# Prompt attention: each unit's two softmax maps are combined between the maxima of the next unit, the first map's sum is carried into the row norm's epsilon, and outputs are copied from PSUM

## The reference

```python
s = einsum('bqhcd,bkhcd->bhcqk', q, k) * scale      # c: the two maps
s = where(dist >= 0, s + bias, -inf)                # causal, ALiBi
p = softmax(s, axis=-1)
a = p[:, :, 0] - lam * p[:, :, 1]
oa = einsum('bhqk,bkhd->bqhd', a, v)
oa = oa * rsqrt(mean(oa * oa, -1) + EPS) * g_oa * (1 - lam_init)
ua = (oa * silu(az)) @ w_branch[0]
```

## Time and profile before

| | us |
|---|---|
| median of 3 runs | 1460.74 |
| lowest, highest | 1460.13, 1461.68 |
| profiled execution, its own time | 1461.76 |
| its span | 1459.8 |
| TensorE busy in the span | 1335.7 |
| VectorE, ScalarE busy | 559.4, 465.2 |

### The profile page before, as it was taken

One profiled execution on the slowest core, in us unless ns is written; L12 is line 12 of the kernel. 1 busy time (PEld: TensorE's weight loads), 2 busy tenths in 40 slices (PEclk: granted clock), 3 DMA queues, 4 the chain that ended last, 5 costly groups with the idle time before them and its releaser, 6 DMA issues.

```text
span 1459.8 us, 19287 instructions
## 1 busy us (share of the span) xinstructions
PE 1335.7 (91%) x7822; PEld 1145.7 (78%) x7822; DVE 559.4 (38%) x1174; ACT 465.2 (32%) x1025; POOL 107.1 (7%) x124
## 2 busy tenths in 40 slices
PE   6999999878787899988769989999999999999998
PEld 5788779656566785867657768778899999999776
DVE  5654334565564324245553334332223222221511
ACT  5543222454444324334442234321222111221300
POOL 0000000000000000000010000000012222221110
PEclk9999999898899999998978989999999999999999
DMA  8340111000002430101111220333111113110422
GB/s 284 112 161 2 58 48 44 15 15 15 0 15 56 159 117 31 30 15 30 44 55 40 62 98 23 109 109 105 44 44 44 44 44 102 44 44 22 144 89 70
DMA packets 89833, 94.41 MB, mean 65 GB/s; under 512 B 8450, under 2 KB 64530, under 8 KB 89618
## 3 DMA queue, kind: packets, MB, share of 16 engines
q1 hardware_dynamic: 85410, 79.28, 17.7%
q0 software_dynamic: 4336, 13.90, 2.6%
HBM read 79.27 MB, written 13.89 MB: 64 GB/s over the span
## 4 chain that ended last, share of the span: by engine, by line
PE 83%; DVE 7%; ACT 6%; issue 4%; DMA 1%; SPq 0%; POOLq 0%; POOL 0%; DVEq 0%; ACTq 0%
PE heavy L813 13%; PE heavy L814 13%; PE heavy L815 13%; PE heavy L825 8%; PE heavy L826 8%; PE heavy L827 8%; PE heavy L870 4%; PE attended L940 2%; ACT arena L1439 2%; PE scores L920 1%; PE transposed L929 1%; PE scores L1173 1%; PE scores L1076 1%; PE transposed L897 1%; PE attended L1190 1%
## 5 line engine op out<-in xcount | busy, mean ns | idle before, releaser
L1332 ACT ACTIVATE arena<-heavy 128x364 f32<-128x364 f32 (+1 forms) x108 | 51.0, 472 | 416.2 <-PE heavy L815 416.2
L813 PE MATMUL heavy<-h_hi,rc_hi 128*128 128x364 f32 (+1 forms) x384 | 134.6, 351 | 2.1 <-DVE arena L2087 2.1
L814 PE MATMUL heavy<-h_lo,rc_hi 128*128 128x364 f32 (+1 forms) x384 | 129.6, 338 | 0.0
L815 PE MATMUL heavy<-h_hi,rc_lo 128*128 128x364 f32 (+1 forms) x384 | 129.3, 337 | 0.0
L813 PE MATMUL heavy<-h_hi,rp_hi 128*128 128x364 f32 (+1 forms) x384 | 126.3, 329 | 0.0
L814 PE MATMUL heavy<-h_lo,rp_hi 128*128 128x364 f32 (+1 forms) x384 | 126.1, 328 | 0.0
L815 PE MATMUL heavy<-h_hi,rp_lo 128*128 128x364 f32 (+1 forms) x384 | 126.1, 328 | 0.0
L1766 DVE SCALAR_TENSOR_TENSOR arena<-arena,heavy 128x364 f32<-128x364 f32 (+1 forms) x48 | 25.5, 532 | 214.1 <-PE heavy L815 214.1
L595 POOL TENSOR_TENSOR merged<-merged,arena 128x364 f32<-128x364 f32 (+1 forms) x48 | 67.1, 1399 | 442.2 <-DVE arena L1766 442.2
L813 PEld LDWEIGHTS heavy<-h_hi,rc_hi 128*128 128x128 f32 x384 | 75.8, 197 | 15.2 <-issue 11.7
L814 PEld LDWEIGHTS heavy<-h_lo,rc_hi 128*128 128x128 f32 x384 | 75.7, 197 | 0.0
(11 more groups left out here) (312 smaller groups left out, 2982.2 us busy)
## 6 DMA issues: line engine op xcount, KB each, us to landing
out<-arena POOLq DMA_DIRECT2D x36, 256.0 KB, 3.3
rc_whole<-w_in SPq DMA_DIRECT2D x16, 512.0 KB, 3.8
rp_whole<-w_in SPq DMA_DIRECT2D x16, 512.0 KB, 4.0
arena<-x_prompt SPq DMA_DIRECT2D x8, 512.0 KB, 5.6
arena<-cache_k_a SPq DMA_DIRECT2D x16, 256.0 KB, 3.0
arena<-cache_v_a SPq DMA_DIRECT2D x16, 256.0 KB, 3.3
ra_whole<-w_in SPq DMA_DIRECT2D x8, 512.0 KB, 4.1
arena<-cache_mem_k SPq DMA_DIRECT2D x8, 512.0 KB, 4.7
```

The source lines that it names most:

```text
L813: nc.tensor.matmul(out, a_hi, b_hi, start=(x == 0), stop=False)
L814: nc.tensor.matmul(out, a_hi, b_lo, start=False, stop=False)
L815: end = nc.tensor.matmul(out, a_lo, b_hi, start=False, stop=(x == len(terms) - 1))
L1332: nc.scalar.activation(tanh[m % 2][:, 0:cw], bank[:, 0:cw], ACT.Tanh, scale=0.5)\
```

## The change

- **Order.** VectorE takes the maximum of map 0 of unit u, combines unit u-1, and takes the maximum of map 1. ScalarE takes the exponentials one by one, each after its own maximum, and in longer units ("long": unit u-1 has more than four key blocks) the first eviction between them. `scores(u)` does map 0 first and waits for each map's reader alone. In long units TensorE's first transposes of unit u-1 stand ahead of the jobs.
- **Arithmetic.** Map 0 is no longer divided by its sum. The weights are p0 - lambda * (sum0 / sum1) * p1, sum0 times what they were; the row norm takes that out again, its epsilon being multiplied by the square of sum0 (`ssum`, `ssq`). So the pass that scaled map 0 is gone, and the combination is done in groups of up to four key blocks, each with its own signal.
- **Tail.** ScalarE copies `attended` to SBUF (`tail_copy`), which alone frees the bank, then squares sum0, squares the four heads from SBUF one after the other, and takes four roots, each with its own epsilon. `tail_scale` works in place, in unit 4(k+1)+3, where the transposes now are too.
- **Jobs.** `FILL_A`: two in units 0 to 3, one in units 4 to 10, 12 to 14, 18, 21, 24, 27, 30, the last after unit 31.

```diff
 NU = H * PT
 A_END = {H * (k + 1) + 1: k for k in range(PT - 1)}
-A_TAIL = {H * (k + 1) + 2: k for k in range(PT - 1)}
+A_TAIL = {H * (k + 1) + 3: k for k in range(PT - 1)}
+FILL_A = [2] * 4 + [1] * 4 + [1, 1, 1, 0] * 2 + [0, 0, 1] * 5 + [0, 1]
 def fill_A(u):
-    js = STAGE["A"]
-    if u < 6:
-        return [js[2 * u], js[2 * u + 1]]
-    n = NU + 1 - 6
-    return [js[12 + x] for x in range(12 * (u - 6) // n, 12 * (u - 5) // n)]
+    return [STAGE["A"][sum(FILL_A[:u]) + x] for x in range(FILL_A[u])]
...
+def weights_of(u, g):
+    return sum(len(groups_A(x)) for x in range(u)) + g + 1
+NA = weights_of(NU - 1, 1)
 
...
+        ssum, ssq, waste = sb("ssum", [P, 2, H]), sb("ssq", [P, H]), sb("waste", [P, P])
...
+        ob_free = sem("ob_free")
...
             def scores(u):
                 i, h = u // H, u % H
                 nk = (i + 1) * P
-                if u:
-                    pe.wait_ge(sc_read, 2 * u)
-                for j in range(0, nk, W):
-                    w = min(W, nk - j)
-                    for c in range(2):
+                for c in range(2):
+                    if u:
+                        pe.wait_ge(sc_read, 2 * (u - 1) + c + 1)
+                    for j in range(0, nk, W):
+                        w = min(W, nk - j)
                         end = nc.tensor.matmul(sc[:, 2 * c + j // W, 0:w], qT[64 * c:64 * c + 64, h, i * P:(i + 1) * P],
                                                kT[64 * c:64 * c + 64, h, j:j + w], start=True, stop=True)
-                        if j + w == nk:
-                            end.then_inc(sc_full, 1)
+                    end.then_inc(sc_full, 1)
 
             def weights_transposed(u, g):
                 b0, b1 = groups_A(u)[g]
+                pe.wait_ge(a_ready, weights_of(u, g))
...
                 if h == 0 and i:
-                    pe.wait_ge(o_free, i)
+                    pe.wait_ge(ob_free, i)
...
+                long = u > 0 and len(groups_A(u - 1)) > 1
+                if long:
+                    weights_transposed(u - 1, 0)
                 for n in fill_A(u):
                     heavy(n)
-                if u:
-                    pe.wait_ge(a_ready, u)
+                if u and not long:
                     weights_transposed(u - 1, 0)
                 if u >= 2:
                     values(u - 2)
-                if u and len(groups_A(u - 1)) > 1:
+                if long:
                     weights_transposed(u - 1, 1)
...
+            def tail_copy(k):
+                act.wait_ge(pv_done, H * (k + 1))
+                if k:
+                    act.wait_ge(tr_full, TRN["tail", k - 1] + 1)
+                nc.scalar.copy(og, OB[:, :]).then_inc(ob_free, 1)
+            def tail_root_A(k):
+                if k:
+                    act.wait_ge(o_free, k)
+                act.wait_ge(ob_free, k + 1)
+                act.wait_ge(p_ready, H * (k + 1))
+                nc.scalar.activation(ssq[:, :], ssum[:, k % 2, :], ACT.Square, scale=EPS ** 0.5)
+                for h in range(H):
+                    settle(nc.scalar.activation(waste[:, :], og[:, h * P:(h + 1) * P], ACT.Square,
+                                                accum_out=ostat[:, 0, h:h + 1]))
+                for h in range(H):
+                    end = nc.scalar.activation(ostat[:, 1, h:h + 1], ostat[:, 0, h:h + 1], ACT.Sqrt,
+                                               bias=ssq[:, h:h + 1], scale=1.0 / P)
+                end.then_inc(oroot_done, 1)
...
-            def exps(u):
-                nk = (u // H + 1) * P
-                act.wait_ge(nmx_ready, u + 1)
-                for c in range(2):
-                    end = nc.scalar.activation(S[u % 2][:, c, 0:nk], S[u % 2][:, c, 0:nk], ACT.Exp,
-                                               bias=nmx[:, c:c + 1], scale=SLOPE[u % H], accum_out=psum_r[:, c:c + 1])
-                end.then_inc(p_ready, 1)
+            def exp_map(u, c):
+                i, h, x = u // H, u % H, 2 * (u % 2) + c
+                nk = (i + 1) * P
+                act.wait_ge(nmx_ready, 2 * u + c + 1)
+                total = ssum[:, i % 2, h:h + 1] if c == 0 else psum_r[:, x:x + 1]
+                end = nc.scalar.activation(S[u % 2][:, c, 0:nk], S[u % 2][:, c, 0:nk], ACT.Exp, bias=nmx[:, x:x + 1],
+                                           scale=SLOPE[h], accum_out=total)
+                if c:
+                    end.then_inc(p_ready, 1)
...
             for u in range(NU):
-                if u:
-                    for n in fill_A(u):
-                        heavy(n)
-                    for g in range(len(groups_A(u - 1))):
-                        weights_evict(u - 1, g)
-                exps(u)
-                if u == 0:
-                    for n in fill_A(u):
-                        heavy(n)
+                long = u > 0 and len(groups_A(u - 1)) > 1
+                exp_map(u, 0)
+                if long:
+                    weights_evict(u - 1, 0)
+                exp_map(u, 1)
+                for n in fill_A(u):
+                    heavy(n)
+                if u and not long:
+                    weights_evict(u - 1, 0)
                 if u in A_END:
-                    tail_root(A_END[u])
+                    tail_copy(A_END[u])
+                if long:
+                    weights_evict(u - 1, 1)
+                if u in A_END:
+                    tail_root_A(A_END[u])
...
-            act.wait_ge(pv_done, NU)
+            tail_copy(PT - 1)
             page_evict(0)
-            tail_root(PT - 1)
+            tail_root_A(PT - 1)
...
-                nc.vector.tensor_tensor(out=og[0:n, :].rearrange("p (x k d) -> p x k d", x=2, k=2), in0=o_rows(k),
+                rows = og[0:n, :].rearrange("p (x k d) -> p x k d", x=2, k=2)
+                nc.vector.tensor_tensor(out=rows, in0=rows if k < TS else o_rows(k),
...
-            def softmax_head(u):
-                nk = (u // H + 1) * P
-                if u >= 2:
+            def softmax_map(u, c):
+                nk, x = (u // H + 1) * P, 2 * (u % 2) + c
+                if u >= 2 and c == 0:
                     dve.wait_ge(tr_full, TRN["a", u - 2, groups_A(u - 2)[-1][0]] + 1)
-                if u:
-                    dve.wait_ge(p_ready, u)
-                for c in range(2):
-                    dve.wait_ge(sc_full, 2 * u + c + 1)
-                    nc.vector.tensor_tensor_reduce(
-                        out=S[u % 2][:, c, 0:nk], in0=distance[:, NP_TOK - nk:NP_TOK],
-                        in1=sc[:, 2 * c:2 * c + 2, :].rearrange("p a n -> p (a n)")[:, 0:nk],
-                        scale=1.0, scalar=NEG, op0=ALU.add, op1=ALU.max,
-                        accum_out=mx[:, c:c + 1]).then_inc(sc_read, 1)
-                dve.wait_ge(sc_read, 2 * u + 2)
-                nc.vector.tensor_scalar(nmx[:, 0:2], mx[:, 0:2], -SLOPE[u % H], None, ALU.mult).then_inc(nmx_ready, 1)
+                dve.wait_ge(sc_full, 2 * u + c + 1)
+                nc.vector.tensor_tensor_reduce(
+                    out=S[u % 2][:, c, 0:nk], in0=distance[:, NP_TOK - nk:NP_TOK],
+                    in1=sc[:, 2 * c:2 * c + 2, :].rearrange("p a n -> p (a n)")[:, 0:nk],
+                    scale=1.0, scalar=NEG, op0=ALU.add, op1=ALU.max,
+                    accum_out=mx[:, x:x + 1]).then_inc(sc_read, 1)
+                dve.wait_ge(sc_read, 2 * u + c + 1)
+                nc.vector.tensor_scalar(nmx[:, x:x + 1], mx[:, x:x + 1], -SLOPE[u % H], None, ALU.mult)\
+                    .then_inc(nmx_ready, 1)
 
             def combine(u):
-                nk = (u // H + 1) * P
+                i, h, x = u // H, u % H, 2 * (u % 2) + 1
                 dve.wait_ge(p_ready, u + 1)
-                settle(nc.vector.reciprocal(coef[:, 0:2], psum_r[:, 0:2]))
-                settle(nc.vector.tensor_scalar(coef[:, 1:2], coef[:, 1:2], neg_lam[:, :], None, ALU.mult))
-                p0, p1 = S[u % 2][:, 0, 0:nk], S[u % 2][:, 1, 0:nk]
-                settle(nc.vector.tensor_scalar(p0, p0, coef[:, 0:1], None, ALU.mult))
-                nc.vector.scalar_tensor_tensor(out=p0, in0=p1, scalar=coef[:, 1:2], in1=p0, op0=ALU.mult,
-                                               op1=ALU.add).then_inc(a_ready, 1)
+                settle(nc.vector.reciprocal(coef[:, 0:1], psum_r[:, x:x + 1]))
+                settle(nc.vector.tensor_scalar(coef[:, 1:2], coef[:, 0:1], ssum[:, i % 2, h:h + 1], neg_lam[:, :],
+                                               ALU.mult, ALU.mult))
+                for b0, b1 in groups_A(u):
+                    p0, p1 = (S[u % 2][:, c, b0 * P:b1 * P] for c in range(2))
+                    nc.vector.scalar_tensor_tensor(out=p0, in0=p1, scalar=coef[:, 1:2], in1=p0, op0=ALU.mult,
+                                                   op1=ALU.add).then_inc(a_ready, 1)
...
             for u in range(NU):
-                softmax_head(u)
+                softmax_map(u, 0)
+                if u:
+                    combine(u - 1)
+                softmax_map(u, 1)
```

(6 more changed lines are left out.)

16 lines of the change are left out of this document (6 added, 10 removed).

## The result

The changed kernel takes 1468.65 us (median of 5 runs, 1466.24 to 1469.97), the kernel before 1460.74: a ratio of 1.0053, 95% interval 1.0041 to 1.0065. It is **slower by 0.5%**; 1450 was forecast, and the range ended at 1465. The profiled execution took 1467.6 us.

A forecast was written before the change was run, and what follows sets the result against it. TensorE's waits (42.1 us) and clock falls (24.5) in prompt attention were taken as the bound. Waits +4.3 and clock -15.7 (falls only at units 11, 15, 22, 26) gave -11.4 us: 1450 us, 8-in-10 range 1438 to 1465.

The forecast's parts named there:

- Part 1: Combination of unit u-1 between the two maxima on VectorE: a new TensorE wait of 1.74 us in 16 units, 27.9 us.
- rival 1: Clock falls at the sixteen short waits, 1.5 to 2.2 us a fall; eight falls give 1467 us; chance 0.15.
- seventh fall: Point from which clock falls at short waits decide: 7 x 2.2 = 15 us, said to cancel the forecast's 11.
- 16 short waits: Units 16 to 31, TensorE before the first transposes, waiting for the combination: 1.74 us each, 27.9 us.
- units 7, 11, 15: TensorE waits after ScalarE's longer root delays jobs and weight splits: 0.9, 3.9 and 3.5 us, together 8.3 us.
- late evictions, units 22, 26: Second transposes wait for ScalarE's first eviction, standing behind the root: 2.6 and 3.3 us, together 5.9 us.
- tail transposes: Tail's transposes wait for the last eviction, now after the second exponential, in units 11, 15, 19, 23, 27: 4.8 us.
- rival 3: ScalarE's root costs no more than before; 10.3 us of waits and up to 4.4 of falls go: 1435 to 1440; chance 0.15.
- one in half of the 16 units: Less favourable end for clock falls at short waits in units 16 to 31: 1.5 to 2.2 us each, 12 to 18 us.
- two rows that spoke against each other: Earlier profile, two TensorE waits of 1.82 us: after 654.12 us the clock stays, after 689.41 it falls to 0.50.
- Part 2: Jobs moved forward, ten instead of eight in units 4 to 15: the 14.2 us of waits in that stretch mostly go.
- Rival 4: VectorE, not TensorE, sets the pace in attention; about no change in time, counted within a shared chance of 0.17.

The follow-up runs named there:

- the row of one map alone: Changed kernel with units 17 to 31 ordered on TensorE as scores of map 0, values of unit u-2, scores of map 1: 1478.84 us.
- three steps of such moves: On the changed kernel with the combination behind both maxima (1452.31): jobs moved, 1450.64; first eviction and tail scaling earlier, 1436.71; second eviction between exponentials, 1432.64 us.
- the kernel with the values first: Changed kernel with the values of unit u-2 ahead of the first transposes of unit u-1 on TensorE in units 17 to 31: 1455.60 us.

## Why the prediction was wrong, step by step

**The step that failed** is in Part 1: "both maps' scores take 1.77 us, so map 1 ends 0.80 us after map 0". The 1.77 us was read as a sum of two, while it is one of two at once; the row of one map alone (1.77) shows it. VectorE's start shows it too: 1.91 us after map 0's scores begin, with map 1 beside them or not. The step took 0.80 us from a wait that is 2.37 to 2.78 us, in 16 units: 41.2 us against 27.9, 13.3 too little. The rest of the chain holds to 0.11 us, most of it the maximum's start, 0.13 us after the scores, not 0.04. The prediction named the condition, "wrong if the short waits are over 2 us (then the clock falls, rival 1)", and so it came. That 1468.65 stands beside rival 1's 1467 is partly luck: the rival has eight falls of 2.2 us, 17.6 us of clock on top of the forecast; measured are 7.0 us of clock on top of it and 13.3 us of longer waits, which the rival doesn't have. Its chance of 0.15 rested on waits of 1.74 us. (Its "seventh fall" is misreckoned: 11.4 us are cancelled by between five and six falls of 2.2 us.)

**The other waits of the sum.**

| term | predicted | measured |
|---|---|---|
| 16 short waits | 27.9 | 41.2 |
| units 7, 11, 15 | 0.9, 3.9, 3.5 | 0.97, 3.98, 3.48 |
| late evictions, units 22, 26 | 2.6, 3.3 | 1.68, 1.71 |
| tail transposes | 4.8 | 4.1 |
| sum | 46.9 | 57.1 |

Units 7, 11 and 15 are right to 0.1 us. The late evictions are shorter for two reasons, seen in unit 26: TensorE itself comes 1.0 us later, 6.6 us after its scores start in place of 5.6, which is mostly the same 0.80 us; and the transposes start 8.4 us after that point in place of 8.9. The 4.1 us of tail transposes aren't where they were put: in the five units named they wait 2.4 us, none of it in unit 11; the rest is 0.98 us in unit 7 and 0.77 us in unit 31. Root with copy takes 6.1 us (404.70 to 410.80) where 5.8 was reckoned, so rival 3 (a root no longer than before) didn't come. ScalarE in unit 25 of the kernel after, in order of time, beside the earlier trace rows:

```profile
404.70 0.56 ACT L1428 COPY arena<-attended 128x512 f32<-128x512 f32 x1
...
405.64 0.30 ACT L1438 ACTIVATE waste<-arena 128x128 f32<-128x128 f32 x1
...
407.35 1.28 ACT L1441 ACT_TABLE_LOAD   x1
408.65 0.85 ACT L1441 ACTIVATE ostat<-ostat,ssq 128x1 f32<-128x1 f32 x4
409.52 1.28 ACT L1469 ACT_TABLE_LOAD   x1
```

**The clock.** Four falls at long waits and none at the short ones were forecast, 8.8 us. There are nine, 31.85 / 2 = 15.9 us, and of the four long waits only unit 11's is followed by one. Eight follow the sixteen short waits, "one in half of the 16 units", as the prediction's less favourable end had it, at 1.6 us each. The forecast had taken the end with no such fall, between two rows that spoke against each other. The gain against before is 24.5 - 15.9 = 8.6 us in place of 15.7, and that is TensorE's 8.7 us less of busy time.

**In all**: waits +15.8 us in place of +4.3, clock -8.7 in place of -15.7, the key page -1.3: +5.8, and the span is 5.9 longer. The error against the forecast's -11.4 is 17.2 us: 13.3 of the short waits, 7.0 of the clock, less 1.8 of the other waits and 1.3 of the key page.

**Part 2** was right in direction; by the run with the old places it is worth 14.4 us, mostly the clock's. **Rival 4** (VectorE sets the pace) didn't come: VectorE itself is idle for 2.50 us ahead of map 0's maximum. What the forecast didn't weigh is that the place of the combination could be judged apart: the other parts, with the combination behind the maxima, give 1452.31.

## What to carry to other kernels

Where two matmul streams use the two halves of the array, time their pair and one alone before reckoning that one is ready first: a pair that costs what one costs gives both results at its end, and a reader of the first can't start sooner than a reader of both. A combination moved ahead of a reader's second pass comes to stand behind its first: if its user on TensorE is the very next instruction, that pass is added to the wait. And when a wait is removed, read which one ends last next (here the exponential, the root, the tail's scaling, the eviction), and move that too; three steps of such moves made 20 us.

## What was not expected of the hardware

- **Fewer matmuls, slower kernel.** Leaving out most of map 1's scores in 16 units cost 12 us, through the clock (88.8 us at 1.2 GHz in place of 34.0), at waits no longer than before.
- **The rows in use mattered to the clock.** The same columns in the same order left 64.8 us of attention at the lower level over 64 rows, 17.0 us over 128. A TensorE busy 96% of 20.6 us stayed at 1.2 GHz. The Trainium skill ("TensorE: Matmul & The Clock Gate", section "What's actually happening") ties the clock to how busy TensorE has been recently; this row doesn't agree with it, if busy is what the profile calls busy.
- **Falls behind short waits.** The clock fell at 384.8 us in the kernel with the values first, behind waits of 0.98, 0.77 and 1.02 us; and after only eight of the sixteen waits of 2.37 to 2.78 us in the changed kernel.
